# The second bank of each turned tile goes from ScalarE to VectorE, and the hand-overs are reordered

## The reference, cut to what matters

```python
h = rms_norm(x, g_mix[l]) * (1.0 + sc_m[:, None]) + sh_m[:, None]
z = h @ w_in[l] + b_in[l]
...
h2 = rms_norm(x, g_ffn[l]) * (1.0 + sc_f[:, None]) + sh_f[:, None]
gate, up = jnp.split(h2 @ w_gu[l], 2, axis=-1)
```

## Time and profile before

| | us |
|---|---|
| median of 3 runs | 3892.98 |
| lowest and highest | 3887.87, 3894.03 |
| the profiled execution: its time, its span | 3886.36, 3884.6 |
| PE busy in the span | 3715.5 (96%) |
| DVE, ACT, POOL busy | 1695.9 (44%), 1448.0 (37%), 1381.6 (36%) |
| chain that ended last, by engine | PE 83%, DVE 8%, ACT 4%, issue 2% |

### The profile page before, as it was taken

The page is one execution under the profiler, slowest core; times in us unless marked ns, Lnnn a source line. Parts: engine busy times, 40 slices in busy tenths (PEclk is TensorE's granted clock), DMA queues, the critical chain, the costliest instruction groups (busy, mean ns, idle before and its releaser), DMA issues.

```text
span 3884.6 us, 67210 instructions
## 1 busy us (share of the span) xinstructions
PE 3715.5 (96%) x28976; PEld 2987.6 (77%) x28976; DVE 1695.9 (44%) x2722; ACT 1448.0 (37%) x2468; POOL 1381.6 (36%) x581
## 2 busy tenths in 40 slices
PE   8888999999999898999999999999999999999999
PEld 7777678788887786688888876578888776688887
DVE  6554541487145554612684158515111377332112
ACT  3454252323324443523223243634222436433222
POOL 5001324344443002144444445234444353234443
PEclk9999999999999999999999999999999999999999
DMA  3001222266221001132473222112222221122222
GB/s 147 3 4 46 84 76 87 87 250 234 87 87 44 4 4 68 66 114 87 161 264 149 87 91 83 44 66 103 104 92 87 108 88 50 60 87 87 87 108 87
DMA packets 37151, 356.66 MB, mean 92 GB/s; under 512 B 4224, under 2 KB 4352, under 8 KB 17920
## 3 DMA queue, kind: packets, MB, share of 16 engines
q1 hardware_dynamic: 19584, 278.93, 19.4%
q10 hardware_dynamic: 17280, 73.48, 5.3%
HBM read 350.29 MB, written 2.10 MB: 91 GB/s over the span
## 4 chain that ended last, share of the span: by engine, by line
PE 83%; DVE 8%; ACT 4%; issue 2%; DMA 1%; PEld 1%; POOL 0%; PEldq 0%; DVEq 0%; SPq 0%; ACTq 0%; POOLq 0%
PE banks L768 23%; PE banks L770 23%; PE banks L769 23%; PE banks L1134 9%; PE banks L2200 3%; ACT arena L2356 2%; ACT arena L1507 2%; DMA ring<-stream 1%; PE banks L2282 1%; DVE arena L1996 1%; PE banks L1261 1%; DVE arena L1891 0%; DVE x L2757 0%; PE banks L1459 0%; DVE arena L2682 0%
## 5 line engine op out<-in xcount | busy, mean ns | idle before, releaser
L866 POOL TENSOR_TENSOR ring_r<-ring,hi_ring 128x1024 fp32r<-128x1024 f32 x490 | 1200.0, 2454 | 2173.5 <-ACT hi_ring L857 2173.4
L768 PE MATMUL banks<-xT_r,ring_r 128*128 128x512 f32 (+1 forms) x2480 | 949.1, 383 | 12.4 <-POOL ring_r L866 6.9
L770 PE MATMUL banks<-xT_r,hi_ring 128*128 128x512 f32 x2096 | 826.3, 394 | 0.0
L769 PE MATMUL banks<-x_lo_r,hi_ring 128*128 128x512 f32 x2096 | 822.0, 392 | 0.0
L857 ACT ACTIVATE hi_ring<-ring 128x1024 fp32r<-128x1024 f32 x490 | 511.3, 1047 | 732.1 <-DMA ring<-stream 314.0
L768 PEld LDWEIGHTS banks<-xT_r,ring_r 128*128 128x128 f32 x2480 | 470.2, 190 | 106.4 <-issue 13.6
L770 PEld LDWEIGHTS banks<-xT_r,hi_ring 128*128 128x128 f32 x2096 | 394.0, 188 | 93.4
L769 PEld LDWEIGHTS banks<-x_lo_r,hi_ring 128*128 128x128 f32 x2096 | 396.0, 189 | 88.1 <-issue 1.4
L1134 PE MATMUL banks<-arena 64*64 64x64 f32 (+4 forms) x7456 | 341.7, 248 | 53.3 <-DVE arena L1891 22.1
L1507 ACT ACTIVATE arena<-banks 128x512 f32<-128x512 f32 x366 | 214.8, 596 | 379.0 <-PE banks L770 221.1
L770 PE MATMUL banks<-hi_ring,pairs 128*128 128x512 f32 x864 | 342.3, 396 | 0.0
(11 more groups left out here) (274 smaller groups left out, 5406.9 us busy)
## 6 DMA issues: line engine op xcount, KB each, us to landing
ring<-stream SPq DMA_DIRECT2D x132, 2048.0 KB, 7.8
arena<-ada ACTq DMA_DIRECT2D x96, 512.0 KB, 4.8
arena<-ln_rows ACTq DMA_DIRECT2D x5, 1024.0 KB, 7.7
arena<-edge ACTq DMA_DIRECT2D x4, 1024.0 KB, 5.1
arena<-edge ACTq DMA_DIRECT2D x2, 1792.0 KB, 7.5
arena<-pack ACTq DMA_DIRECT2D x2, 1485.0 KB, 6.9
arena<-pack ACTq DMA_DIRECT2D x2, 1200.5 KB, 5.5
x<-x_in SPq DMA_DIRECT2D x4, 512.0 KB, 7.5
```

What stands on the lines that cost most here:

```text
L768: first = nc.tensor.matmul(out_, left[1], right[0], start=start, stop=False)
L769: low = nc.tensor.matmul(out_, left[0], right[1], start=False, stop=False)
L770: return first, low, nc.tensor.matmul(out_, left[0], right[0], start=False, stop=stop)
L866: nc.gpsimd.tensor_tensor(feed.raw(n, ring_r), feed.raw(n), feed.hi(n).bitcast(F32), ALU.subtract).then_inc(split_lo, 1)
```

## The change

For bank 1 of each turned tile ACT's four scale-and-shift instructions go. DVE does them as two of 128x512: a multiplication from the bank by the scale, spread over the 128 tokens of each square, and an addition of the shift, both into `x_lo_value`. A new semaphore, `turned_mod`, tells ACT to make the rounded copy of that half. On DVE both stand where `turn2` stands in the program. ACT's copy and what is behind it in its list now wait for DVE. The lists in `apart` are also written anew.

```diff
--- before.py
+++ after.py
@@ -364,19 +364,18 @@
             return [names.get(name, lambda n: (name, (0, n)))(n) for name, n in what]
         opened = [("rows_open", ("qa",))]
         if k == L:
-            early[2:] = [of(("split", 0)), of(("square", 0), ("rms", 0)), of(("scaled", 0), ("split", 1), ("split", 2)),
-                         of(("square", 1), ("rms", 1), ("turn2", 0), ("low2", 0)), of(("scaled", 1), ("split", 3)), [],
-                         opened + of(("turn2", 1), ("square", 2), ("rms", 2), ("low2", 1), ("qa", 0)),
-                         of(("scaled", 2), ("turn2", 2), ("low2", 2), ("qa", 1), ("square", 3), ("rms", 3), ("scaled", 3), ("out", 0),
+            early[2:] = [of(("split", 0)), of(("square", 0), ("rms", 0)), of(("scaled", 0), ("split", 1)),
+                         of(("square", 1), ("rms", 1), ("turn2", 0), ("low2", 0)), of(("scaled", 1), ("split", 2), ("split", 3)), [],
+                         opened + of(("turn2", 1), ("low2", 1), ("square", 2), ("rms", 2), ("qa", 0)),
+                         of(("scaled", 2), ("square", 3), ("rms", 3), ("turn2", 2), ("low2", 2), ("qa", 1), ("scaled", 3), ("out", 0),
                             ("split", 4), ("split", 5), ("turn2", 3), ("low2", 3), ("split", 6), ("qa", 2), ("out", 1), ("qa", 3),
                             ("out", 2))]
         else:
-            early[2:] = [[], of(("square", 0), ("rms", 0)), of(("scaled", 0)), of(("square", 1), ("rms", 1)),
-                         of(("split", 0), ("scaled", 1), ("square", 2), ("split", 1)), of(("turn2", 0)),
-                         opened + of(("split", 2), ("split", 3), ("turn2", 1)),
-                         of(("rms", 2), ("low2", 0), ("square", 3), ("low2", 1), ("rms", 3), ("scaled", 2), ("qa", 0), ("turn2", 2),
-                            ("low2", 2), ("scaled", 3), ("qa", 1), ("out", 0), ("split", 4), ("split", 5), ("turn2", 3), ("low2", 3),
-                            ("split", 6), ("qa", 2), ("out", 1), ("qa", 3), ("out", 2))]
+            early[2:] = [[], of(("square", 0), ("rms", 0)), of(("scaled", 0)), of(("square", 1), ("rms", 1)), of(("split", 0)),
+                         of(("turn2", 0)), opened + of(("split", 1), ("low2", 0), ("scaled", 1), ("split", 2), ("split", 3)),
+                         of(("turn2", 1), ("low2", 1), ("square", 2), ("rms", 2), ("square", 3), ("rms", 3), ("scaled", 2), ("qa", 0),
+                            ("turn2", 2), ("low2", 2), ("scaled", 3), ("qa", 1), ("out", 0), ("split", 4), ("split", 5), ("turn2", 3),
+                            ("low2", 3), ("split", 6), ("qa", 2), ("out", 1), ("qa", 3), ("out", 2))]
     return early, [s_ for s_ in steps if s_ not in sum(early, [])]
 
 
@@ -758,6 +757,7 @@
     hid_hi = sem("hid_hi")
     hid_lo = sem("hid_lo")
     turned_hi = sem("turned_hi")
+    turned_mod = sem("turned_mod")
     branch_hi = sem("branch_hi")
     branch_lo = sem("branch_lo")
     merged_hi = sem("merged_hi")
@@ -2393,13 +2393,15 @@
                 if (which, tt) == (0, 0):
                     act.wait_ge(params2_ready, 1)
                 for i in range(2):
-                    filled(banks[i], use[i])
-                    for k in range(4):
-                        d = 4 * i + k
-                        ins = f(dst[:, d, tt * P:(tt + 1) * P], bank[banks[i]][:, k * P:(k + 1) * P], ACT.Identity,
-                                bias=mod_of[layer][:, 24 * which + d:24 * which + d + 1], scale=gain[:, 8 * which + d:8 * which + d + 1])
                     here = slice(4 * i, 4 * i + 4), slice(tt * P, (tt + 1) * P)
-                    link(ins)
+                    if i == 0:
+                        filled(banks[0], use[0])
+                        for k in range(4):
+                            ins = f(dst[:, k, tt * P:(tt + 1) * P], bank[banks[0]][:, k * P:(k + 1) * P], ACT.Identity,
+                                    bias=mod_of[layer][:, 24 * which + k:24 * which + k + 1], scale=gain[:, 8 * which + k:8 * which + k + 1])
+                        link(ins)
+                    else:
+                        act.wait_ge(turned_mod, which * TT + tt + 1)
                     f(x_pair[0][:, here[0], here[1]], dst[:, here[0], here[1]], ACT.Copy).then_inc(turned_hi, 1)
             elif name in ("split", "hid_split"):
                 if name == "split" and args[0] == 0:
@@ -2755,10 +2757,17 @@
                     .then_inc(bank_free[b_], 1)
                 again(b_, n_)
                 V.tensor_tensor(x_tok[:, tt, cols_], x_tok[:, tt, cols_], t, ALU.add).then_inc(x_added, 1)
-            elif name == "low2" or (name == "turn2" and args[0] == 1):
+            elif name in ("low2", "turn2"):
                 which, tt = args
-                banks = uses[("turn2", which, tt)][0]
-                for i in range(2):
+                banks, use = uses[("turn2", which, tt)]
+                if name == "turn2":
+                    filled(banks[1], use[1])
+                    second = x_lo_value[:, 4:8, tt * P:(tt + 1) * P]
+                    scale, shift = [a.unsqueeze(2).to_broadcast([P, 4, P]) for a in (gain[:, 8 * which + 4:8 * which + 8],
+                                                                                    mod_of[layer][:, 24 * which + 4:24 * which + 8])]
+                    link(V.tensor_tensor(second, bank[banks[1]][:, :].rearrange("p (k s) -> p k s", k=4), scale, ALU.mult))
+                    V.tensor_tensor(second, second, shift, ALU.add).then_inc(turned_mod, 1)
+                for i in range(2) if name == "low2" or which == 1 else ():
                     dve.wait_ge(turned_hi, 2 * (which * TT + tt) + i + 1)
                     here = slice(4 * i, 4 * i + 4), slice(tt * P, (tt + 1) * P)
                     V.tensor_tensor(x_pair[1][:, here[0], here[1]], x_lo_value[:, here[0], here[1]],
...
@@ -2807,7 +2816,7 @@
...
-                      (gt_ready, 4), (params2_ready, 1), (square_done, 2 * TT), (xn_ready, 2 * TT), (row_stats, TT), (row_power, TT), (staged, 1), (sums_sq, 1 + 2 * TT), (roped, len(staged_order)),
+                      (gt_ready, 4), (params2_ready, 1), (square_done, 2 * TT), (xn_ready, 2 * TT), (row_stats, TT), (row_power, TT), (turned_mod, 2 * TT), (staged, 1), (sums_sq, 1 + 2 * TT), (roped, len(staged_order)),
```

## The result

The changed kernel takes 3892.94 us (median of 22 runs, 3888.07 to 3906.05), the kernel before beside it 3889.27 (22 runs, 3880.88 to 3894.03): ratio 1.0016, interval 1.0010 to 1.0022, so 6.2 us slower (3.9 to 8.6). The two medians are only 3.7 apart; the ratio on record is not that of the medians. The loss is within the 0.2% that the prediction counts as no change, and its interval leaves out 1. The predicted difference was +2.7.

The account below looks back on a forecast made before the run. PE is busy 96% of the span, so only its waits around the 16 turns can change (17.4 us at transposes). Terms 0.7 + 1.2 + 0.8 = +2.7 on 3892.98 give 3895.7 us; likeliest case 3888 to 3901, 8 in 10 3884 to 3903.

Parts of the forecast that it names:

- PSUM read not held, SBUF addition held, though its second input is four numbers: DVE's new pair: multiplication always 0.69 us; addition 0.69, or beside POOL the rest of its instruction plus 0.6.
- The second rival: POOL does not hold the new additions: -1.4, -0.5 twice and -0.7, together -3.1 us, 3889.9; chance 22%.
- the bound without low clock: Entry stretch: with no clock loss, the next transposes start at 2276.1, -1.4 us.
- The added wait: At tile 1, ACT's copy and the squares queued behind it wait for DVE; ACT idles about 3 us.
- Entry, +0.7 forecast: Entry stretch: tile 2's transposes 1.0 us late, the next at 2278.2 against 2277.49; bounds -1.4 to +2.0.
- Inner, +0.6 each: Both inner stretches: tile 3's transposes start 0.6 us later, 1.2 together; bounds -0.5 to +1.2 each.
- Between, +0.8 forecast with a bound of 2.4: Between the blocks: next transposes +0.1 us, or +1.6 if DVE falls behind one more piece; +0.8 taken, bounds -0.7 to +2.4.
- The first rival: Inner stretches and between: tile 1's additions each held by one further POOL piece; +10.4 us, 3903.4; chance 12%.
- The third: The path shortens at every turn by up to 1.4 us, ten waits, 14 us: 3879; chance 10%.
- low clock for more than 6 us in a stretch: Sign that the forecast is wrong: PE's clock low for longer than 6 us in any stretch.

Follow-up runs that it names:

- experiment 5: Changed kernel, but DVE's multiplication writes its product back into the PSUM bank and the addition reads it there; ratio 0.9996 to the kernel before.
- experiment 2: Changed kernel with ACT doing both banks as before, the new lists kept; ratio 0.9998 to the kernel before.
- experiment 1: Changed kernel with the old lists, except tile 0's low parts between the blocks one place earlier; ratio 1.0021 to the kernel before.
- 7: Changed kernel, but DVE does the second bank only in the inner stretches, ACT both banks elsewhere; ratio 1.0005 to the kernel before.
- 9: Changed kernel with the product kept in the PSUM bank, and ACT doing both banks in the entry stretch; ratio 0.9990, 3884.79 us against 3886.83 before.
- experiment 8: Changed kernel, but DVE does the second bank only between the blocks, in four one-pass instructions from PSUM, ACT both banks elsewhere; ratio 0.9995 to the kernel before.
- experiment 6: Changed kernel, but DVE does the second bank only at the entry and between the blocks, ACT both banks in the inner stretches; ratio 1.0012 to before.
- 3: Changed kernel, but DVE makes the second bank in four one-pass 128x128 multiply-and-add instructions from PSUM, new lists; ratio 1.0000 to the kernel before.
- 4: Changed kernel with four one-pass DVE instructions from PSUM and the old lists, tile 0's low parts between the blocks one place earlier; ratio 1.0007 to before.

## Why the prediction was near, and where it was off

The mechanism was right; its three terms, 0.7, 1.2 and 0.8, were all too small. The nearness of the absolute time (3895.7 for 3892.94) owes something to luck: the kernel before had a median of 3889.27 in the runs beside the changed one, 3.7 below the one that the prediction started from. The difference, +2.7, was off by 3.5 against the ratio and by 1.0 against the two medians.

- **PSUM read not held, SBUF addition held, though its second input is four numbers.** Right, and shown by experiment 5. The second rival, additions not held, is what experiment 5 makes of the kernel: it priced that at -0.5 for an inner stretch (-0.45 and -0.59 measured) and -0.7 between (-0.85), but -1.4 at the entry, where it is +1.15. That price was wrong in itself. The forecast's replay of the entry already had both additions at 0.69, so without holds it stays at +0.7; the -1.4 is the bound without low clock, which has nothing to do with holds, and added up right it is 2270.15 + 6.45 = 2276.6, -0.9.
- **The added wait.** Right in place and size: ACT idles 3.45 at tile 1 in the entry stretch, 2.90 inner, 3.75 between. PE's wait before the entry's third transposes is 3.66 (3 to 4 forecast), the one before its fourth is gone, and in the inner stretches tile 3's transposes wait 3.41 once (3.5 forecast).
- **Entry, +0.7 forecast, +1.8.** The term is that of tile 2's transposes: 1.0 late was forecast, 2.3 it is (19.38 for 17.08). Square 2 stood where the replay had it (15.1 behind the first transposes, 15.0 forecast), although the addition of 2269.23 had caught the end of a POOL piece (1.33). Behind it, 1.0 is POOL's power, held in its turn by DVE; the replay took 1.95 us from square 2 to the scaled tile, where the rows of before have 2.42 (2265.49 to 2267.91, power 0.93) and the changed kernel 3.04. This comes with the new order and not with DVE's share: the power takes 1.52 in experiment 2 and 0.93 with the old lists in 1. By experiments 7 and 9, whose new lists and low clock give 38.75, the lists account for +0.7 of the 1.8. DVE's share without the hold adds 0.45 (39.21 in experiment 5), the holds 0.64 more.
- **Inner, +0.6 each, +1.2 and +0.8.** Square 2 came where the replay had it (13.95 behind the first transposes, 13.83 forecast). The eight transposes behind the 3.41 us wait then ran at the low clock, which the forecast had only as a bound. In the first stretch most of it is only moved: before, the low clock fell on the products behind the stretch's end, and past it +0.2 is left of the +1.2. In the second the spell is also longer, +1.6 past it, and that need not be the change, since experiment 8 has it too. A window of the first:

```profile
2714.00:2716.00 2.00, 2.00 (x10) 1.99 (x11) 0.67 (x2) 0.91 (x3) 0.00 (x0) 0.50 0.00 0
```

- **Between, +0.8 forecast with a bound of 2.4, +3.1.** The step that failed. Tile 1's first transposes came when forecast (7.0 behind the first; 7.1). But the step counted tile 0's low parts at their short length; POOL's three pieces held one of them, and the second four transposes stood 2 us later. Tile 2's transposes came 18.7 behind the first; the replay had 17.4, and 18.1 with the +0.8 that it took. The second spell of low clock cost a further 1.6, for which the forecast and its bound had nothing; it is the larger part of the miss. The holds are worth 2.3 (37.53 in experiment 6 against 35.28 in 5), the second spell 1.7 (39.19 against 37.53). Holds and new order make this together: with the old lists the stretch is 36.09 in spite of the held addition.
- **The first rival, slower by holds of one further piece**, came true only between the blocks, as a chain of held instructions and a second spell of low clock. The third, a shorter path at every turn, is excluded: no wait went without another coming.
- The sign "low clock for more than 6 us in a stretch" came true and says little: between the blocks the spell lasted about 6.8 us before already.

The new lists alone are worth nothing that can be measured (0.9998). Their stretch between is 0.6 shorter, their entry 0.8 shorter or 0.7 longer, as the clock falls.

## What to carry to other kernels

When work moves to an engine that shares something with a third, price it by what it reads, not by its size: here the same addition is 0.69 us from PSUM and up to 2.2 from SBUF beside GpSimd, and moving one operand brought back what the change had lost. Such a hold costs most where several instructions of a chain fall under back-to-back work of the other engine, so follow the whole chain under it, the old instructions too. And where PE idles for 2 to 4 us at a hand-over, put the low clock behind it into the sum as likely and not as a bound: here it came in 8 of the 10 entry stretches of the changed kernel and the experiments, whose waits were 2.4 to 3.8 us.

## What the runs showed of the hardware

- An input spread from four numbers a partition counts as a full SBUF input: held up to 2.20 us in the changed kernel, 2.56 in experiment 6 and 2.87 in experiment 1, 0.69 otherwise.
- The hold is whole, not a slowing: a held instruction of 128x512 with both inputs in SBUF ends 0.54 to 0.56 us after POOL's running piece does, in all eleven profiles, however early it began.
- The hold works both ways. POOL's 128x1 instruction, 0.55 us at its shortest, took 1.52 to 1.57 when it began inside DVE's two-input instruction of 1.28, in every profile; begun inside one of DVE's that reads PSUM, it was never longer than 0.6. No experiment was made for this.
- Which engine is held is decided by hundredths: DVE's scaled tile took 2.95 to 2.98 in the four cases where it began at most 0.01 us ahead of POOL's piece (experiments 3 and 4), and 0.75 or 0.76 in the other eighteen, where it began 0.05 us or more ahead; then POOL's piece lasted longer instead, up to 2.97 for 2.42. These rows of DVE and POOL are from experiment 5:

```profile
2692.61 0.75 DVE L2580 TENSOR_SCALAR arena<-x,small 128x1024 f32<-128x1024 f32 x1 [0.66 <-POOL small L2529]
```

```profile
2692.66 5.79 POOL L866 TENSOR_TENSOR ring_r<-ring,head 128x1024 fp32r<-128x1024 f32 x2
```

- After the same wait of 2.4 us PE's clock stayed at 2.4 GHz in experiments 2 and 8, and fell to 1.2 GHz for some 3.4 us in 7 and 9.
